# First stage of a block kernel: adds of the modulation pieces placed apart, other orders of transfers, filter work and weight halves

## What is computed

```python
cond = jax.nn.silu(c)
mod = (cond @ w_ada[l] + b_ada[l])[:, None, :]           # 2048 x 12288 weights, one row of input
sh1, sc1, g1, sh2, sc2, g2 = jnp.split(mod, N_MOD, axis=-1)
h = x * (1.0 + sc1) + sh1
z = h @ w_in[l] + b_in[l]                                # first columns of it: z_u, z_v
...
h = jnp.sin(fr * (feats @ w1 + b1)); h = jnp.sin(fr * (h @ w2 + b2)); h = h @ w3
window = jnp.exp(-t * deltas)                            # filters = h * window
k_spec = jnp.fft.rfft(k, axis=0)                         # done as products with a DFT table
```

## Time and profile before

| What | Value |
|---|---|
| time, median of 3 runs | 2631.37 us (2631.11 to 2634.38) |
| time of the profiled execution | 2630.96 us |
| its span | 2629.6 us |
| mean granted TensorE clock | 0.997 of full speed |
| TensorE busy | 2597.2 us, 99% of the span |
| VectorE busy | 1845.6 us, 70% |
| ScalarE busy | 1289.7 us, 49% |

### The profile page before, as it was taken

The page is one execution under the profiler, slowest core; times in us unless marked ns, Lnnn a source line. Parts: engine busy times, 40 slices in busy tenths (PEclk is TensorE's granted clock), DMA queues, the critical chain, the costliest instruction groups (busy, mean ns, idle before and its releaser), DMA issues.

```text
span 2629.6 us, 31620 instructions
## 1 busy us (share of the span) xinstructions
PE 2597.2 (99%) x12546; PEld 2169.0 (82%) x12546; DVE 1845.6 (70%) x1927; ACT 1289.7 (49%) x1566; POOL 32.1 (1%) x55
## 2 busy tenths in 40 slices
PE   7999999999999999999999999999999999999999
PEld 3789988878888888888888888888888888988887
DVE  9978989988876644687776767756554665666565
ACT  2455444444444444555555544444444654545463
POOL 0000000000000000000000000000000000000000
PEclk9999999999999999999999999999999999999999
DMA  9998877798688755666555665555655556634554
GB/s 399 382 371 303 305 283 286 273 338 315 238 297 283 247 185 188 193 204 203 192 192 193 192 191 177 192 190 184 211 192 192 183 185 172 177 125 160 192 177 143
DMA packets 276584, 598.65 MB, mean 228 GB/s; under 512 B 21264, under 2 KB 46288, under 8 KB 260064
## 3 DMA queue, kind: packets, MB, share of 16 engines
q1 hardware_dynamic: 268272, 566.52, 63.2%
q0 software_dynamic: 4560, 21.56, 2.5%
q10 hardware_dynamic: 3616, 8.68, 0.8%
HBM read 586.24 MB, written 10.49 MB: 227 GB/s over the span
## 4 chain that ended last, share of the span: by engine, by line
PE 89%; DVE 7%; DMA 2%; issue 1%; ACT 1%; ACTq 0%; DVEq 0%; SPq 0%
PE ps L951 26%; PE ps L953 26%; PE ps L952 26%; DVE group_acc L2390 2%; PE ps L1076 2%; DVE w_lo L2271 2%; PE ps L1060 2%; PE ps L1063 1%; PE ps L1062 1%; DMA raw<-in_k_in 1%; PE ps L1461 1%; PE ps L1463 1%; PE ps L1462 1%; DMA raw<-in_w_in 1%; DVE ada_acc L2299 1%
## 5 line engine op out<-in xcount | busy, mean ns | idle before, releaser
L2271 DVE TENSOR_TENSOR w_lo<-raw,w_hi 128x1024 fp32r<-128x1024 f32 x870 | 1050.3, 1221 | 663.0 <-ACT w_hi L1607 661.0
L1607 ACT CAST w_hi<-raw 128x1024 fp32r<-128x1024 f32 x870 | 906.8, 1051 | 1074.5 <-PE ps L953 900.2
L951 PE MATMUL ps<-w_lo,x_hi 128*128 128x512 f32 x2592 | 1019.5, 393 | 6.6 <-DVE w_lo L2271 2.8
L953 PE MATMUL ps<-w_hi,x_lo 128*128 128x512 f32 x2592 | 1010.7, 390 | 0.0
L952 PE MATMUL ps<-w_hi,x_hi 128*128 128x512 f32 x2592 | 1010.0, 390 | 0.0
L951 PEld LDWEIGHTS ps<-w_lo,x_hi 128*128 128x128 f32 x2592 | 487.4, 188 | 111.9 <-DVE w_lo L2271 4.6
L953 PEld LDWEIGHTS ps<-w_hi,x_lo 128*128 128x128 f32 x2592 | 487.1, 188 | 102.1
L952 PEld LDWEIGHTS ps<-w_hi,x_hi 128*128 128x128 f32 x2592 | 487.6, 188 | 99.8 <-issue 1.0
L2299 DVE SCALAR_TENSOR_TENSOR ada_acc<-raw,cond,ada_acc 128x2048 f32<-128x2048 f32 x64 | 150.1, 2345 | 2.5 <-DMA raw<-in_w_ada 1.5
L951 PE MATMUL ps<-w_lo,pooled_hi 128*128 128x512 f32 x384 | 150.3, 391 | 0.0
L953 PE MATMUL ps<-w_hi,pooled_lo 128*128 128x512 f32 x384 | 149.5, 389 | 0.0
(11 more groups left out here) (379 smaller groups left out, 2135.9 us busy)
## 6 DMA issues: line engine op xcount, KB each, us to landing
raw<-in_w_m SPq DMA_DIRECT2D x128, 1024.0 KB, 5.2
raw<-in_w_ada SPq DMA_DIRECT2D x64, 1024.0 KB, 6.0
raw<-in_pool_w_in SPq DMA_DIRECT2D x64, 1024.0 KB, 5.3
raw<-in_w_in SPq DMA_DIRECT2D x56, 1024.0 KB, 7.3
raw<-in_k_mod SPq DMA_DIRECT2D x32, 1024.0 KB, 7.3
raw<-in_pool_w_out SPq DMA_DIRECT2D x32, 1024.0 KB, 5.0
raw<-in_ple_w_gate SPq DMA_DIRECT2D x32, 1024.0 KB, 5.1
raw<-in_mla_w_in SPq DMA_DIRECT2D x24, 1024.0 KB, 5.1
```

The lines of the kernel that those rows point to most:

```text
L951: mm(bank, xh, wl, start=start, stop=False)
L953: ins = mm(bank, xl, wh, start=False, stop=stop)
L1607: nc.scalar.copy(by_ktile(st, w_hi[st.half_slot(j, half)][:, 0:n]), raw_half(st, j, half)).then_inc(hi_split, 1)
L2271: tt(by_ktile(st, w_lo[slot][:, 0:n]), raw_half(st, j, half), by_ktile(st, w_hi[slot][:, 0:n].bitcast(F32)), ALU.subtract).then_inc(lo_spl ...
```

## The change

It touches the first stage and the hooks around the start of `in_h`; no arithmetic is added or dropped. Five things:

1. `add_first` is made of two `add_half(q, u, e)`, each of which now signals `group_added` itself, so that waits count to 16 a group and not to 8. In seven pieces, (1,2), (1,7), (2,2), (2,5), (3,1), (3,2) and (3,3), something else now stands between the two adds. In the rest of the list the whole order of VectorE is another one.
2. SyncE's order: `w3` and the DFT table go earlier, weight units take other places among the pieces, `x` of group 1 comes before that of group 0, and the bias row of chunk 0 moves from behind the last unit to the middle of group 3.
3. TensorE does `filter_product(1, 0)` and `(1, 1)` before the first spectrum, and puts spectra and units in another order. Units (2,0) and (2,1), and (3,1) and (3,2), change places.
4. ScalarE rounds in the order of the units, forms `x_hi` of group 3 before it stores the first spectrum, and has other moments for the stores, the loads of small columns and the GELUs.
5. On VectorE `vu_out(0)` goes behind the two halves of the last unit, `vu_out(3)` behind one more `add_ada`, and the moments and the split of the DFT table stand 1 and 3 halves later in `in_h`.

```diff
-    ("first", 1, [("ggggggggwggg", ""), ("wgggggggggwg", ""), ("wggwggwwgwgw", ""), ("ggwwgggwwww", "")]),
+    ("first", 1, [("ggggwggggggg", ""), ("ggggwggwgggw", ""), ("ggwwggwggwgw", ""), ("gwggwggwwww", "")]),
...
-                    sync.wait_ge(group_added, used_g)
+                    sync.wait_ge(group_added, 2 * used_g)
...
-        def add_first(q, u):
+        def add_half(q, u, e):
 
             st, j = ST["first"], group_ada(q, u)
-            dve.wait_ge(raw_full[st.slot(j)], st.landed(0, j))
-            if u:
-                dve.wait_ge(group_added, 8 * q + u)
+            if e == 0:
+                dve.wait_ge(raw_full[st.slot(j)], st.landed(0, j))
+            if u + e:
+                dve.wait_ge(group_added, 16 * q + 2 * u + e)
             elif q >= 2:
                 dve.wait_ge(group_summed, q - 1)
             buf = group_acc[q % 2]
...
+            ins.then_inc(group_added, 1)
+
+        def add_first(q, u):
+
             for e in range(2):
...
+                add_half(q, u, e)
...
         add_first(3, 0)
-        group_rest(1, 2)
-        group_rest_half(0, 3, 0)
         group_scale(2)
-        add_first(3, 1)
         group_rest_half(0, 3, 1)
+        add_half(3, 1, 0)
+        group_lo(2, 0)
+        add_half(3, 1, 1)
+        group_rest(2, 0)
...
         act.wait_ge(half_used, first_half(1, 3, 1))
         nc.scalar.copy(part_u[:], ps[:, 6:8, :]).then_inc(part_kept, 1)
         group_round(2, 3)
+        group_hi(3, 0)
+        group_round(3, 0)
+        group_hi(3, 1)
+        group_round(3, 1)
         spectrum_store(0)
-        group_round(3, 0)
-        group_hi(3, 0)
...
-        def in_h_8():
+        def in_h_0():
+            gelu(0)
+            gelu(1)
+
+        def in_h_3():
+            gelu(2)
+            round_dft(0)
+
+        def in_h_11():
+            gelu(3)
             spectrum_store(3)
...
         def in_h_2():
+            add_ada(ST["in_vu"], 0, 2, 2, 1)
             vu_out(3)
-            add_ada(ST["in_vu"], 0, 2, 2, 1)
```

234 lines of the change are left out of this document (117 added, 117 removed).

## The result

| | before | after |
|---|---|---|
| median of the timed runs, 8 each | 2632.95 us (2631.11 to 2634.67) | 2640.07 us (2637.88 to 2645.63) |
| ratio | | 1.0031, 95% interval 1.0021 to 1.0040 |
| time of the profiled execution | 2630.96 us | 2640.79 us |
| its span, mean granted clock | 2629.6 us, 0.997 | 2639.5 us, 0.994 |

The change makes the kernel slower by 0.31%, some 8 us (7.1 us between the two medians), where 2628.5 us (2624.5 to 2632.0) was forecast. The profiled execution of before lies 2.0 us under its median of 2632.95 and that of after 0.7 us above its own, so of the 9.8 us between the two profiled ones some 2 to 3 are luck.

What follows compares the result with a forecast made beforehand. VectorE's add chain was taken to bind up to the fourth group sum, TensorE behind 136.7 us. Terms -1.6 + 0.6 + 0 - 1.9 = -2.9 us on 2630.96 gave 2628.1, with 0.4 for the median 2628.5 us; range 2624.5 to 2632.

Steps and rivals of the forecast that it cites:

- the add chain ahead of it: First stage: VectorE's adds, ending at 134.4 us, were said to bound the kernel until TensorE does from 136.7 us.
- The adds placed apart: First stage, VectorE: breaking links between neighbouring adds was to save 1.6 us, bounds 0 and 1.6.
- The bias row: First stage transfers: chunk 0's 256 KB row, now ahead of the last pieces, was to cost 0.6 us.
- VectorE's waits unchanged: First stage: VectorE's 4.2 us of waits for casts were to stay as they were, 0, bounds -4.2 and +4.2.
- TensorE ready at 130.9 us: Fourth group sum: TensorE was to be ready some 3.7 us before 134.56, so its new order costs nothing.
- less slack was named as a sign of error: Fourth group sum: TensorE was to wait over 2 us; no wait there would mean the prediction is wrong.
- From the group sum on: Group sum to 165.7 us: same count of work, stage ends 1.0 us earlier, half clock's 1.7 us kept, bounds -1.7 and +1.7.
- The start of in_h: First 25.2 us of in_h: TensorE's 1.9 us lost in three waits for w_lo were to go, -1.9 us.
- the new hooks spread this: Start of in_h: the third w_lo wait, behind add_ada, moments and three GELUs of 2.95 us, was to be relieved.
- The rivals: Alternatives: VectorE's waits go, 2625.8 us (0.20); split gains nothing, 2630.1 (0.13); in_h gaps move, 2630.4 (0.14); slower case (0.05).
- The ring at the third group sum: First stage: late spectrum_out(3, 1) delays TensorE, VectorE and loads in turn; 2631.7 us if once, 2638.1 if passed on; chance 0.05.

Runs made afterwards that it cites:

- before_w22_late: The kernel before with weights (2,2) one place later in transfers and on VectorE, two pieces behind them instead of three: ratio 0.9993.
- before_in_h_after: The kernel before, first stage unchanged, with all of the change's in_h helpers (stores, GELUs, LayerNorm, small loads): 2636.78 us, ratio 1.0015.

## Why the prediction was wrong

**What bounds the kernel.** Right for the matmul rate behind the stage. Half right in "the add chain ahead of it": VectorE's splits and adds bind only from the landing of weights (2,2) on, the last 8.7 us (11.4 in the old order, the cast included). Ahead of that landing the stream of transfers binds, at a DMA share of 0.96 to 0.97, and VectorE stands 1.6 us for it at that place.

**The adds placed apart, -1.6 us.** The price of a link was read rightly: the add at 88.28 has its next instruction 1.19 us later, linked pairs are 1.31 apart. But all seven links that it breaks stand ahead of a wait for a landing, where a shorter chain only waits longer. Joined or apart the ratio is 1.0010. The term should have been 0, its own lower bound. By the rule of the Trainium skill that the prediction draws on ("VectorE: DVE Perf Modes", section "The DRAIN you can't avoid") it is 0 too, the right sum for another reason: that page of the Trainium skill measured it on copies, and the same section lets an instruction that isn't held start earlier, as the 1.19 us here do. (Of "the next three pairs of adds" ahead of the rows of the change only two have a row of `x_lo` between them; the third, (3,3), has a `w_lo`.)

**The bias row, +0.6 us.** Its bytes are in the account of the landings; alone it measured 1.0005 on the kernel before (1.3 us, an interval that includes 1) and nothing on the changed one.

**VectorE's waits unchanged, 0 (bounds -4.2 to +4.2).** This is the first step that failed. They were 8.2 us for casts and 1.7 for pieces in the profiled execution: +5.7, beyond the bound, with the group sum at 138.84 for the 133.6 forecast. The text noted that "four slots and some 7.3 us from issue to landing are as before" and took that for the landings too. They were not: the last piece came at 134.95 for 130.44, weights (2,2) at 130.01 for 123.02. One place where the new list holds a slot is plain, the add behind a half whose cast is not yet done, for which SyncE waits 6.1 us; but taking it out alone left the sum late (137.33), and only with the bias row put back as well did it return to 134.9 to 135.4. How the two act together stays open.

**TensorE ready at 130.9 us, no cost.** Wrong: it reached the sum at 138.2, 0.7 us early, since weights (2,2) were cast only from 130.03 on. It cost nothing that the times show (before_w22_late, with 0.2 us of slack, 0.9993), and less slack was named as a sign of error.

**From the group sum on.** As forecast, 31.1 us with the half clock kept.

**The start of in_h, -1.9 us (bounds 0 and +1.1).** The mechanism worked at the place it spoke of: in the first 24 us the difference to before falls from 4.3 to 3.2 us. The step that failed is what it left out: "the new hooks spread this" prices the GELUs and leaves out the store that moved with them, and what waits for that store. Its loss was 3.56 us and a half-clock stretch, 5.2 us in all, and LayerNorm's new step another 0.3 to 1.1 us in the profiled executions; they lie 40 and 27 us behind the start of `in_h`, beyond the 25 us looked at. The rule to count a moved step's transfers would have found it: in the old trace the store takes 11.9 us from issue (181.27) to landing (193.12), and `z_fm` already waits 2.3 us for it, starting at 193.23. Moved some 8 us later, it could only get worse.

**The sum against the trace.** 2640.79 us is 12.7 us above the 2628.1 forecast for a profiled execution. Of these, 5.2 had arisen by the group sum (138.84 for 133.6), 0.8 at the start of `in_h` (a gain of 1.1 for 1.9), 5.6 from there to 214 us, nearly all of it the store, and 1.1 between 460 and 570 us.

**The rivals.** None of them was it. The ring at the third group sum cost a wait of 0.6 us for `spec_out`. A slot held up by a late cast was there, but at another place, around 88 us behind weights (1,0), and no kernel shows that this alone cost time.

**What stays open.** Why transfers take longer between 58 and 94 us in the new order (on average 35.7 us for 12.25 MB; 34.1 us for 12.0), why a late store alone is free in the kernel before, and why bias row and add together put the profiled group sums right (three of three), which neither did alone, while the first such kernel was still at 1.0013; with LayerNorm's 0.0008 taken off that is 0.0005, inside the interval, but the 0.0008 is itself not resolved.

## What to carry to other kernels

When a list of helpers is spread anew, follow each transfer in it to the one who waits for its landing, with the trace's own time from issue to landing, and look past the stretch in which the gain is expected. Where DMA engines are full and slots few, look for the last landing that an engine really waits for, and take the work behind it as a fixed tail: the end of the stage is that landing plus the tail. Count bytes ahead of it, and look at each load for the instruction that frees its slot and for what that instruction now stands behind. Shortening the chain ahead of that wait is worth nothing; behind it, here, it could be worth up to 1.1 us, the time that the last piece lies ready before its first add (an estimate; no kernel here tried it).

## What the runs showed of the hardware

- The stream of transfers has slow spells, some of them at the same time of the span whichever unit is in flight. In each of the twenty executions the landings between 80 and 86.5 us were late by 0.6 to 3.0 us in all, though the units that pass then differ between old and new order; outside such spells landings mostly follow each other by 2.48 us per MB to within 0.05. In sum the spells come to 8 to 12 us up to the last piece. I found nothing else in the profile that marks these times.
- A half-clock stretch of 3.4 us or more (1.2 GHz) follows the fourth group sum in 15 of 20 executions. The wait in front of the sum doesn't tell whether it comes: it was 0 to 3.4 us long where it came and 0.2 to 0.8 us where it didn't. One of 3.4 us costs 1.5 us: 31.1 us against 29.6 for the same 120 matmuls and what lies before them. Whether it makes much of the scatter in the total is open: in the old order the four profiled executions without it took 2631.93 to 2635.18 us and three with it 2630.96 to 2633.73 (the fourth, before_in_h_after, has the late store besides); 33 runs of the kernel before lay between 2628.42 and 2637.94 us.
